# Residual sums that stay on the chip as the next layer's input, with their squares; normalisation moved into the next projection, chunk by chunk; the first token mixture in two VectorE passes

## The chip, the cores and the metric

The kernel runs on one core of one Trainium2 chip. The metric is the time of one execution on the device in microseconds (us); of three runs of the kernel before, the median is 6700.87 us.

## What is computed

Four layers work on 256 context tokens and 1024 latent tokens of 1024 channels in float32. The layers' mixers are RWKV-7 (layer 0), neighbourhood attention (layer 1), S5 (layer 2) and RWKV-7 again (layer 3). Around each mixer:

```python
for i in range(DEPTH):
    hx = _rms_norm(x, norm_g[i]) * (1.0 + scale_x) + shift_x
    hc = _rms_norm(ctx, norm_g[i]) * (1.0 + scale_c) + shift_c
    ...                                    # oc, ox = mixer(hc, hx)
    x = x + gate_x * ox
    if need_ctx:
        ctx = ctx + gate_c * oc
```

`_rms_norm` divides by the root of the mean square over the channels. Scale, shift and gate come from a modulation matrix and differ between context and latents. The RWKV mixer starts with six mixtures of each token with its neighbours: `xx = _centred_shift(h) - h` (the centred shift is half the sum of the left and the right neighbour), then `xs = h + xx * mu[n]` for n = 0 to 5, each followed by a projection.

## The kernel before

Channels lie on the 128 partitions in eight tiles (KT = 8), the 1280 tokens (T) along the free axis, the context first (SEGS). Matmuls work on three chunks of tokens, (0,512), (512,1024), (1024,1280) (CHUNKS), one PSUM bank each. In the last layer the first and the fourth projection need latents alone and use two chunks from token 256. The program is a row of phases. Each phase (class Phase, L57) opens a block in which every engine has its own instruction list, ordered by semaphores, and ends with a barrier of all engines (L83) and the clearing of its semaphores by GpSimd (L89). Nothing of the next phase starts before that barrier.

One layer runs through these phases. In RWKV layers `load_constants` (L112) loads eight small tensors. `norm` (L298) loads the residual stream from DRAM into h (SP, L312), squares each tile on ScalarE (L320), adds the squares over channels on TensorE with a matrix of ones (L337), forms the reciprocal root by Ln and Exp on ScalarE (L322, L324), multiplies h by it on VectorE (L348) and applies scale and shift on ScalarE (L328, once for the context and once for the latents). In layers 0 and 3 TensorE's list also has 147 and 17 instructions at its end that do nothing but count a semaphore (NORM_FILL). Then a projection phase multiplies h with strips of weights of 128 output channels: `rwkv_project` (L1580), `na_project` (L534) or `s5_prepare` (L950). Then the mixer (`rwkv_recur`, `na_attention`, or S5's scan and outputs), and at last `dense_residual` (L459), which multiplies the output with eight strips (L356), adds the gated product to the residual on VectorE (L507), and stores the sum to DRAM (L515). Its loop is a hardware loop of four turns with two strips each on every engine.

In `rwkv_project` VectorE prepares the first mixture group by group: neighbour sums (L1638), edge columns (L1642), `dd = 0.5*sum - h` (L1645) and `xs[0] = h + dd*mu` (L1631); after each group TensorE may use that chunk (xs_part, L1679). The five other mixtures are whole passes over 1280 columns. GpSimd in the meantime weighs the next layer's modulation strips (class HiddenModulation, L132; L153, L156), also in the projections of layers 1 and 2. In layer 3 there is no next layer and GpSimd is idle.

In `s5_prepare` VectorE and ScalarE work out the discretised states (L1176 to L1223 and on) while TensorE multiplies the first eight strips. In `na_project` SP loads eight pieces of value weights (L557) before the first two strips (L561). In `rwkv_recur` TensorE runs a loop over eight channel tiles, with an inner loop of five windows, both in hardware loops.

## Time and profile before

| | |
|---|---|
| runs | 6700.87 us median, 6697.97 to 6701.71 |
| span of the profiled execution | 6691.4 us |
| TensorE matmuls busy | 5726.3 us, 86% |
| VectorE busy | 2945.0 us, 44% |
| ScalarE busy | 2000.7 us, 30% |
| GpSimd busy | 1877.3 us, 28% |
| mean granted TensorE clock | 0.932 |
| HBM read and written | 329.14 MB, 105.87 MB |

The span is cut into phases by the barriers. Within it, a layer's norm phase is recognised by SP's eight loads of L312, and the following phase by its first instruction. The engines are named PE (TensorE), DVE (VectorE), ACT (ScalarE), POOL (GpSimd) and SP; a name with a q is the engine's sequencer or queue. A float32 matmul appears as two records.

### The profile page before, as it was taken

The page shows a single profiled execution, that of the slowest core. Times are in us where ns is not written, and L with a number is a line of the kernel's source. Part 1 is how long each engine was busy: PE and PEld are TensorE (multiplying, and loading weights), DVE is VectorE, ACT ScalarE, POOL GpSimd, SP SyncE. Part 2 cuts the span into 40 slices and gives each one's busy share as a digit, 9 for nine tenths or more (in the row PEclk, how much of TensorE's full clock was granted, in tenths as well). Part 3 has the DMA queues.
Part 4 walks back from the last instruction along what each step waited for, and adds up shares of the span by engine and source line. Part 5 has one row for each costly group of instructions (what it writes and reads, how often), then busy time and mean ns, then how long its engine had stood idle before and what let it go on. Part 6 is the DMA issues. An engine that isn't in the chain of part 4 may idle for free. (4 is left out here: it accounts for less than half of the span.)

```text
span 6691.4 us, 214952 instructions
## 1 busy us (share of the span) xinstructions
PE 5726.3 (86%) x92840; PEld 3836.5 (57%) x92840; DVE 2945.0 (44%) x6319; ACT 2000.7 (30%) x3323; POOL 1877.3 (28%) x2006
## 2 busy tenths in 40 slices
PE   5999888888887799977887885689799888888887
PEld 4555577777774355445554453544354477777773
DVE  6200266666662233135533377520310366666661
ACT  1000255555440222133422132310100254555440
POOL 4452144444441335100001641000000244444440
PEclk8999999999998899988898997899899899999998
DMA  3222100001102322122212236523112100011002
GB/s 125 89 96 82 50 31 31 31 33 43 37 31 85 121 76 97 46 85 64 62 48 103 97 104 92 122 73 115 52 68 75 47 31 31 31 44 39 31 31 91
DMA packets 196092, 441.22 MB, mean 66 GB/s; under 512 B 24769, under 2 KB 108609, under 8 KB 195649
## 3 DMA queue, kind: packets, MB, share of 16 engines
q1 hardware_dynamic: 160896, 338.58, 17.0%
q10 hardware_dynamic: 34752, 96.51, 3.6%
q8 instruction: 304, 4.98, 0.3%
q14 instruction: 140, 1.14, 0.1%
HBM read 329.14 MB, written 105.87 MB: 65 GB/s over the span
## 5 line engine op out<-in xcount | busy, mean ns | idle before, releaser
L356 PE MATMUL ps<-arena 128*128 128x512 f32 x4544 | 1683.6, 532 | 73.1 <-DMA arena<-s_w_in 27.4
L356 PEld LDWEIGHTS ps<-arena 128*128 128x128 f32 x4544 | 862.3, 190 | 889.7 <-issue 853.9
L1875 PE MATMUL ps<-arena 64*64 64x64 f32 x35840 | 741.3, 225 | 164.2 <-DVE arena L2542 66.1
L153 POOL TENSOR_TENSOR arena<-arena 128x512 f32<-128x512 f32 (+1 forms) x360 | 330.6, 935 | 1782.7 <-DMA arena<-w_mod 1772.5
L1875 PEld LDWEIGHTS ps<-arena 64*64 64x64 f32 x35840 | 646.8, 138 | 237.9 <-issue 223.9
L2280 ACT COPY arena<-ps 128x512 f32<-128x512 f32 (+1 forms) x880 | 536.0, 627 | 426.6 <-PE ps L1875 418.3
L2425 POOL TENSOR_TENSOR arena<-arena 128x256 f32<-128x256 f32 (+1 forms) x320 | 318.5, 1002 | 807.7 <-DVE arena L2666 528.9
L570 PE MATMUL ps<-arena 128*128 128x512 f32 (+1 forms) x1152 | 424.2, 528 | 33.5 <-DMA arena<-na_w_in 33.5
L2350 POOL MEMSET arena<- 128x1280 f32 (+4 forms) x22 | 15.1, 739 | 1370.6 <-POOLq L83 1370.6
L1631 DVE SCALAR_TENSOR_TENSOR arena<-arena 128x1280 f32<-128x1280 f32 (+3 forms) x120 | 147.2, 1299 | 567.2 <-PE ps L356 477.1
L156 POOL TENSOR_TENSOR arena<-arena 128x256 f32<-128x256 f32 (+2 forms) x504 | 381.8, 769 | 52.0 <-issue 2.1
L1696 ACT COPY arena<-ps 128x1280 f32<-128x1280 f32 (+1 forms) x64 | 75.0, 1172 | 1054.3 <-PE ps L356 749.0
L2542 DVE TENSOR_TENSOR arena<-ps,arena 128x512 f32<-128x512 f32 x486 | 319.5, 686 | 91.0 <-PE ps L1862 42.3
L570 PEld LDWEIGHTS ps<-arena 128*128 128x128 f32 x1152 | 219.9, 191 | 227.1 <-issue 215.9
L1679 PE MATMUL ps<-arena 128*128 128x512 f32 (+1 forms) x640 | 260.0, 568 | 96.2 <-DVE arena L1631 96.2
L507 DVE SCALAR_TENSOR_TENSOR arena<-ps,arena 128x1024 f32<-128x1024 f32 (+1 forms) x56 | 50.5, 937 | 507.4 <-PE ps L356 507.4
L1843 PE MATMUL ps<-arena 128*128 128x512 f32 (+1 forms) x432 | 225.9, 629 | 37.5 <-DMA arena<-rw_par 36.4
L653 DVE RECIPROCAL arena<-arena 128x1280 f32<-128x1280 f32 x16 | 130.5, 8154 | 288.2 <-ACT arena L615 288.2
L1679 PEld LDWEIGHTS ps<-arena 128*128 128x128 f32 x640 | 124.3, 195 | 230.3 <-issue 206.0
L2613 DVE TENSOR_TENSOR arena<-ps,arena 128x512 f32<-128x512 f32 x240 | 165.4, 689 | 166.7 <-ACT arena L2280 100.1
L2703 DVE SCALAR_TENSOR_TENSOR arena<-ps,arena 128x64 f32<-128x64 f32 x576 | 136.2, 278 | 227.6 <-PE ps L2089 218.1
L320 ACT ACTIVATE arena<-arena 128x1280 f32<-128x1280 f32 x32 | 40.6, 1270 | 593.3 <-DMA arena<-xres 489.7
(258 smaller groups left out, 9853.6 us busy)
## 6 DMA issues: line engine op xcount, KB each, us to landing
arena<-proj SPq DMA_DIRECT2D x158, 640.0 KB, 5.1
proj<-arena ACTq DMA_DIRECT2D x80, 640.0 KB, 4.0
arena<-w_mod SPq DMA_DIRECT2D x96, 512.0 KB, 7.6
arena<-rw_w SPq DMA_DIRECT2D x68, 512.0 KB, 3.7
arena<-xres SPq DMA_DIRECT2D x40, 640.0 KB, 6.7
xres<-arena ACTq DMA_DIRECT2D x24, 640.0 KB, 6.0
arena<-na_w_in SPq DMA_DIRECT2D x24, 512.0 KB, 3.5
arena<-x SPq DMA_DIRECT2D x16, 640.0 KB, 6.6
```

The source lines that it names most:

```text
L153: self.nc.gpsimd.tensor_tensor(out, strip[:, c:c + n, :], self.k.cond[:, c:c + n, s:s + 1].to_broadcast([P, n, P]), ALU.mult)
L156: self.nc.gpsimd.tensor_tensor(out, a, b, ALU.add)
L356: last = nc.tensor.matmul(k.ps[:, 3 * u + n, 0:b - a], w[:, c * P:(c + 1) * P], src[:, c, a:b], start=(c == 0), stop=(c == KT - 1))
L570: last = PE.matmul(k.ps[:, 3 * (s % 2) + n, 0:b - a], strips_[:, s % 2, c * P:(c + 1) * P], h[:, c, a:b], start=(c == 0), stop=(c == KT - 1))
L1631: return V.scalar_tensor_tensor(xs[n % 2][:, c, a:b], dd[:, c, a:b], k.mu[:, (j * 6 + n) * KT + c:(j * 6 + n) * KT + c + 1], h[:, c, a:b], ...
L1679: last = nc.tensor.matmul(k.ps[:, 3 * u + m, 0:b - a], strips_[:, u, c * P:(c + 1) * P], xs[0][:, c, a:b], start=(c == 0), stop=(c == KT - 1))
L1843: PE.matmul(lora_bank(banks, i), w2t[:, 2 * which + s, :], hid[:, which, a:b], start=True, stop=True).then_inc(lora_mm, 1)
L1875: last = PE.matmul(part_of(out, dst, hh, g, d), part(l, src, hh, g, d), rhs, start=True, stop=True)
L2280: SC.copy(out, in_).then_inc(ev, 1)
L2425: return GP_.tensor_tensor(eighths(out), eighths(in_), k.eye2.unsqueeze(1).to_broadcast([P, out.shape[1] // C, C]), ALU.add)
L2542: return V.tensor_tensor(out.rearrange("p (h g q) -> p h g q", h=2, g=2), in_.rearrange("p h (g q) -> p h g q", g=2), flat(mask).unsqueeze ...
L2613: return V.tensor_tensor(out.rearrange("p (h q c) -> p h q c", h=2, c=C), in_.rearrange("p h (q c) -> p h q c", c=C), k.eye2.unsqueeze(1). ...
```

## The change

Four things change together.

1. `dense_residual` writes the residual sum into k.h, a fixed place at the top of SBUF that is kept until the next projection; it still stores it to DRAM, since the next residual addition reads it there. In the first three layers ScalarE squares each finished tile and VectorE adds it into k.acc (T columns). The hardware loop is written out as eight strips.
2. The norm phases and their loads are gone, and NORM_FILL with them. Ahead of layer 0 a new phase `first_squares` loads x into k.h and sums its squares in the same way, before the constants of the layer are loaded.
3. The class Normalised runs at the head of each projection phase: three matmuls with ones over k.acc, then Ln and Exp for each of three pieces of tokens, the multiplications on VectorE and scale and shift on ScalarE piece by piece. TensorE waits for a piece before the first strip's chunk of it (attention and S5); in RWKV VectorE waits before its neighbour sums. A piece in RWKV is one token longer where a neighbour is needed.
4. In RWKV the first mixture is `xs[0] = (1-mu)*h` on ScalarE, then `xs[0] += (mu/2)*sum` on VectorE. `dd = 0.5*sum - h` is made after all groups, in one pass over 1280 columns. The tile block hid now shares one tile with dd, so ScalarE waits for the sixth mixture before it writes hid.

```diff
-NORM_FILL = {0: 147, 3: 17}
...
+class Normalised:
+    def __init__(self, nc, k, es, layer, pieces):
+        self.nc, self.k, self.layer, self.pieces = nc, k, layer, pieces
+        self.sums, self.root, self.scaled, self.ready = (es.semaphore("nm_" + n) for n in ("sums", "root", "scaled", "ready"))
+    def tensor_part(self, pe):
+        for a, b in CHUNKS:
+            self.nc.tensor.matmul(self.k.psf[:, 3 * BANK + a:3 * BANK + b], self.k.ones, self.k.acc[:, a:b], start=True, stop=True).then_inc(self.sums, 1)
+    def scalar_roots(self, act):
+        for a, b in self.pieces:
+            act.wait_ge(self.sums, len(CHUNKS))
+            rstd = self.k.acc[:, a:b]
+            self.nc.scalar.activation(rstd, self.k.psf[:, 3 * BANK + a:3 * BANK + b], ACT.Ln, bias=self.k.eps, scale=1.0 / D)
+            act.drain()
+            self.nc.scalar.activation(rstd, rstd, ACT.Exp, scale=-0.5).then_inc(self.root, 1)
+    def vector_part(self, dve, m):
+        a, b = self.pieces[m]
+        dve.wait_ge(self.root, m + 1)
+        for c in range(KT):
+            h = self.k.h[:, c, a:b]
+            self.nc.vector.tensor_tensor(h, h, self.k.acc[:, a:b], ALU.mult).then_inc(self.scaled, 1)
+    def scalar_part(self, act, m, c):
+        a, b = self.pieces[m]
+        act.wait_ge(self.scaled, m * KT + c + 1)
+        for s, (lo, hi) in enumerate(SEGS):
+            lo, hi = max(lo, a), min(hi, b)
+            if lo < hi:
+                h = self.k.h[:, c, lo:hi]
+                last = self.nc.scalar.activation(h, h, ACT.Identity, bias=self.k.mod[:, self.layer * MODS + c, s:s + 1],
+                                                 scale=self.k.mod[:, self.layer * MODS + 8 + c, s:s + 1])
+        return last.then_inc(self.ready, 1)
+    def wait_ready(self, eng, m, c=KT - 1):
+        eng.wait_ge(self.ready, m * KT + c + 1)
+def first_squares(nc, k, src):
...
-        @block.tensor
-        def _(pe):
-            for c in range(KT):
-                pe.wait_ge(sq_done, c + 1)
-                for n, (a, b) in enumerate(CHUNKS):
-                    last = nc.tensor.matmul(k.ps[:, n, 0:b - a], k.ones, sq[:, c % 2, a:b],
-                                            start=(c == 0), stop=(c == KT - 1))
-                last.then_inc(mm_done, 1)
-            for _ in range(NORM_FILL.get(layer, 0)):
-                hold(k, pe)
+                    act.wait_ge(added, c - 1)
+                nc.scalar.activation(sq[:, c % 2, :], k.h[:, c, :], ACT.Square).then_inc(sq_done, 1)
         @block.vector
         def _(dve):
-            dve.wait_ge(root_done, 1)
             for c in range(KT):
-                dve.wait_ge(x_in[c], 16)
-                nc.vector.tensor_tensor(h[:, c, :], h[:, c, :], rstd, ALU.mult).then_inc(scaled, 1)
-def strip_matmuls(nc, k, u, w, src, chunks=CHUNKS):
+                dve.wait_ge(sq_done, c + 1)
+                if c == 0:
+                    nc.vector.tensor_copy(k.acc, sq[:, 0, :]).then_inc(added, 1)
+                else:
+                    dve.wait_ge(added, c)
+                    nc.vector.tensor_tensor(k.acc, k.acc, sq[:, c % 2, :], ALU.add).then_inc(added, 1)
+def strip_matmuls(nc, k, u, w, src, chunks=CHUNKS, before=None):
 
     for n, (a, b) in enumerate(chunks):
+        if before:
+            before(n)
         for c in range(KT):
...
+            for c in range(KT):
+                u = c % 2
+                if c >= 2:
+                    sp.wait_ge(mm_done, c - 1)
+                sp.dma_start(strips[:, u, :], weights[c]).then_inc(w_in[u], 16)
+                if c >= 2:
+                    sp.wait_ge(ev_done, c - 1)
+                sp.dma_start(xin[:, u, first:T], src[c][:, first:T]).then_inc(x_in[u], 16)
 
...
+            def add_squares(c):
+                dve.wait_ge(sq_done, c + 1)
+                if c == 0:
+                    nc.vector.tensor_copy(k.acc, sq[:, 0, :]).then_inc(added, 1)
+                else:
+                    dve.wait_ge(added, c)
+                    nc.vector.tensor_tensor(k.acc, k.acc, sq[:, c % 2, :], ALU.add).then_inc(added, 1)
+
+            for c in range(KT):
+                u = c % 2
+                dve.wait_ge(mm_done, c + 1)
+                dve.wait_ge(x_in[u], c // 2 * 16 + 16)
+                for s, (a, b) in list(enumerate(SEGS))[int(latents):]:
+                    gate = k.mod[:, layer * MODS + 16 + c, s:s + 1]
+                    out, prod, x = k.h[:, c, a:b], acc(k, u)[:, a - first:b - first], xin[:, u, a:b]
+                    if chunked:
+                        out, x = (v.rearrange("p (j s) -> p j s", s=S) for v in (out, x))
+                        prod = acc(k, u).rearrange("p (s j) -> p j s", s=S)[:, a // S:b // S, :]
+                    last = nc.vector.scalar_tensor_tensor(out, prod, gate, x, ALU.mult, ALU.add)
+                last.then_inc(ev_done, 1)
+                if c and not latents:
+                    add_squares(c - 1)
+            if not latents:
+                add_squares(KT - 1)
 
...
+            for c in range(KT):
+                act.wait_ge(ev_done, c + 1)
+                act.dma_start(dst[c], k.h[:, c, first:T]).then_inc(stored, 16)
+                if not latents:
+                    if c >= 2:
+                        act.wait_ge(added, c - 1)
+                    nc.scalar.activation(sq[:, c % 2, :], k.h[:, c, :], ACT.Square).then_inc(sq_done, 1)
+            act.wait_ge(stored, 16 * KT)
...
+            normal.tensor_part(pe)
+
             def chunk(s, n):
                 a, b = CHUNKS[n]
+                if s == 0:
+                    normal.wait_ready(pe, n)
...
+            normal.scalar_roots(act)
+            for m in range(len(CHUNKS)):
+                for c in range(KT):
+                    normal.scalar_part(act, m, c)
...
+            for m in range(len(CHUNKS)):
+                normal.vector_part(dve, m)
...
+            normal.scalar_roots(act)
             act.wait_ge(par_in, 128)
             SC.activation(step, step, ACT.Exp).then_inc(stepped, 1)
+            for m in range(len(CHUNKS)):
+                for c in range(KT):
+                    normal.scalar_part(act, m, c)
...
+            for m in range(len(CHUNKS)):
+                normal.vector_part(dve, m)
...
+    groups = chunks_of(0) + [(0, tokens_of(0))][:tokens_of(0)]
+    kept_mixed = len(chunks_of(0))
+    pieces = [(a + (a > 0 and a != tokens_of(0)), b + (b < T and b != NCTX)) for a, b in groups]
...
+            mu = k.mu[:, j * 6 * KT:(j * 6 + 1) * KT]
+            V.tensor_scalar(half_mu, mu, 0.5, None, ALU.mult)
+            V.tensor_scalar(less_mu, mu, -1.0, 1.0, ALU.mult, ALU.add)
+            dve.drain().then_inc(mu_split, 1)
             edges = [t for a, b in SEGS for t in ((a, a + 1), (b - 1, b - 2))]
-            for a, b in chunks_of(0) + [(0, tokens_of(0))][:tokens_of(0)]:
+            normal.vector_part(dve, 0)
+            for m, (a, b) in enumerate(groups):
                 lo, hi = max(a, 1), min(b, T - 1)
                 for c in range(KT):
+                    normal.wait_ready(dve, m, c)
                     V.tensor_tensor(dd[:, c, lo:hi], h[:, c, lo - 1:hi - 1], h[:, c, lo + 1:hi + 1], ALU.add)
                 dve.drain()
                 for t, beside in edges:
                     if a <= t < b:
                         V.tensor_copy(dd[:, :, t:t + 1], h[:, :, beside:beside + 1])
                 dve.drain()
-                for c in range(KT):
-                    V.scalar_tensor_tensor(dd[:, c, a:b], dd[:, c, a:b], 0.5, h[:, c, a:b], ALU.mult, ALU.subtract)
-                dve.drain()
-                if a >= tokens_of(0):
+                if m < kept_mixed:
                     for c in range(KT):
-                        last = mix(0, c, a, b)
+                        dve.wait_ge(kept_part, m * KT + c + 1)
+                        last = V.scalar_tensor_tensor(xs[0][:, c, a:b], dd[:, c, a:b], half_mu[:, c:c + 1], xs[0][:, c, a:b], ALU.mult, ALU.add)
                     last.then_inc(xs_part, 1)
+                if m + 1 < len(groups):
+                    normal.vector_part(dve, m + 1)
+            dve.drain()
+            for c in range(KT):
+                V.scalar_tensor_tensor(dd[:, c, :], dd[:, c, :], 0.5, h[:, c, :], ALU.mult, ALU.subtract)
+            dve.drain()
...
+            normal.scalar_roots(act)
+            act.wait_ge(mu_split, 1)
+            for m, (a, b) in enumerate(groups):
+                for c in range(KT):
+                    normal.scalar_part(act, m, c)
+                if m < kept_mixed:
+                    act.wait_ge(normal.ready, (m + 1) * KT)
+                    for c in range(KT):
+                        nc.scalar.activation(xs[0][:, c, a:b], h[:, c, a:b], ACT.Copy, scale=less_mu[:, c:c + 1]).then_inc(kept_part, 1)
...
+            act.wait_ge(xs_ready, 5)
...
+        first_squares(nc, k, src)
...
```

The rest of the diff moves addresses in SBUF, takes the removed arguments out of calls and deletes `dense_to_dram`, which nothing calls.

## Rows read from the trace of the kernel before

**Rows 1.** Waits of TensorE, whole span: total us, times, longest us

```profile
PE ps L337 <- ACT arena L320: 49.8, 4, 16.1
```

**Rows 2.** Timeline, layer 0 to 1: start us, us, engine, line, operation, out<-in, [idle <-releaser]

```profile
2212.01 1.68 DVE L507 SCALAR_TENSOR_TENSOR arena<-ps,arena 128x256 f32<-128x256 f32 x2 [15.35 <-PE ps L356]
...
2217.30 4.62 SPq L312 DMA_DIRECT2D arena<-xres  x8
...
2247.24 13.10 ACT L328 ACTIVATE arena<-arena 128x256 f32<-128x256 f32 x16 [1.56 <-DVE arena L348]
2260.59 4.79 SPq L557 DMA_DIRECT2D arena<-na_w_v  x8
...
2275.15 5.47 PE L570 MATMUL ps<-arena 128*128 128x512 f32 x6 [33.45 <-DMA arena<-na_w_in]
```

**Rows 3.** Timeline of ACT, squares of the norm phase of layer 1

```profile
2226.72 1.27 ACT L320 ACTIVATE arena<-arena 128x1280 f32<-128x1280 f32 x1 [2.26 <-PE ps L337]
2228.87 1.27 ACT L320 ACTIVATE arena<-arena 128x1280 f32<-128x1280 f32 x1 [0.89 <-PE ps L337]
```

**Rows 4.** Timeline of ACT, roots of the same norm phase

```profile
2241.73 1.33 ACT L322 ACTIVATE arena<-ps,arena 128x1280 f32<-128x1280 f32 x1 [1.68 <-PE ps L337]
2243.11 1.28 ACT L324 ACT_TABLE_LOAD   x1
2244.41 1.27 ACT L324 ACTIVATE arena<-arena 128x1280 f32<-128x1280 f32 x1
```

**Rows 5.** Groups by form, 4650 to 4762 us: busy us, mean ns of one, idle

```profile
L348 DVE TENSOR_TENSOR arena<-arena 128x1280 f32<-128x1280 f32 x8 | 11.3, 1488 | 38.2 <-ACT arena L324 38.2
L1631 DVE SCALAR_TENSOR_TENSOR arena<-arena 128x512 f32<-128x512 f32 x16 | 10.8, 746 | 0.2
...
L328 ACT ACTIVATE arena<-arena 128x1024 f32<-128x1024 f32 x8 | 9.8, 1226 | 0.0
...
L328 ACT ACTIVATE arena<-arena 128x256 f32<-128x256 f32 x8 | 4.7, 586 | 1.6 <-DVE arena L348 1.6
```

**Rows 6.** Timeline, layer 1 to 2: norm loads and first projection matmuls

```profile
3589.20 0.83 SPq L312 DMA_DIRECT2D arena<-xres  x2
...
3641.14 36.97 PE L356 MATMUL ps<-arena 128*128 128x512 f32 x96 [27.42 <-DMA arena<-s_w_in]
```

**Rows 7.** Timeline, layer 2 to 3: norm loads and TensorE's second chunk

```profile
4666.55 4.15 SPq L312 DMA_DIRECT2D arena<-xres  x8
...
4742.20 28.20 PE L1679 MATMUL ps<-arena 128*128 128x512 f32 x58 [6.10 <-DVE arena L1631]
```

**Rows 8.** Timeline around layer 0: SP, DVE, GpSimd and TensorE

```profile
72.84 0.34 SPq L120 DMA_DIRECT2D arena<-m_x  x1
...
78.55 4.20 SPq L312 DMA_DIRECT2D arena<-x  x8
...
124.04 4.89 DVE L1638 TENSOR_TENSOR arena<-arena 128x511 f32<-128x511 f32 x8 [4.76 <-PEq L83]
...
155.68 5.52 POOL L156 TENSOR_TENSOR arena<-arena 128x256 f32<-128x256 f32 x5
...
168.48 30.75 PE L1679 MATMUL ps<-arena 128*128 128x512 f32 x80 [13.32 <-DVE arena L1631]
```

**Rows 9.** Stretch of layer 0's norm: us, engines busy, PEclk, DMA share, GB/s

```profile
92.00:94.00 2.00, 2.00 (x7) 1.08 (x6) 0.00 (x0) 1.11 (x2) 0.00 (x0) 1.00 0.44 182
```

**Rows 10.** Groups by form, 78 to 200 us: neighbour sums beside GpSimd

```profile
L1638 DVE TENSOR_TENSOR arena<-arena 128x512 f32<-128x512 f32 x8 | 9.3, 1226 | 0.0
```

**Rows 11.** Timeline of DVE, evictions of layer 0's residual (third in rows 2)

```profile
2177.60 1.68 DVE L507 SCALAR_TENSOR_TENSOR arena<-ps,arena 128x256 f32<-128x256 f32 x2 [15.35 <-PE ps L356]
2194.98 1.68 DVE L507 SCALAR_TENSOR_TENSOR arena<-ps,arena 128x256 f32<-128x256 f32 x2 [15.71 <-PE ps L356]
```

**Rows 12.** DMA queues, one tile of the recurrence, 1047 to 1201 us: packets, MB

```profile
q8 instruction: 14, 0.23, 0.7%
```

**Rows 13.** Waits of TensorE in the same tile

```profile
PE ps L1875 <- issue: 5.1, 8, 2.3
```

More of the change, by code:

```diff
@@ L40, in __init__, with hold_h @@
     def __init__(self, tensor, cols):
-        self.tensor, self.cols, self.at = tensor, cols, 0
+        self.tensor, self.all, self.cols, self.at = tensor, cols, cols, 0
+    def hold_h(self, held):
+        self.cols = self.all - KT * T * held
     def take(self, *shape):
@@ L300, in norm @@
+def first_squares(nc, k, src):
     sq = k.arena.take(2, T)
-    rstd = k.arena.take(T)
     with Phase(nc) as es:
-        sem = lambda n: es.semaphore(n)
-        x_in = [sem(f"x_in{c}") for c in range(KT)]
-        sq_done, mm_done, root_done = sem("sq_done"), sem("ss_mm"), sem("root_done")
-        scaled, final = sem("scaled"), sem("final")
+        x_in = [es.semaphore(f"x_in{c}") for c in range(KT)]
+        sq_done, added = es.semaphore("sq_done"), es.semaphore("sq_added")
         block = es.block()
@@ L478, in _ @@
         def _(sp):
-            with sp.Fori(0, n) as i:
-                for u in range(2):
-                    sp.wait_ge(mm_done[u], i + 1)
-                    sp.dma_start(strips[:, u, :], dram_tile(weights, i * 2 + u)).then_inc(w_in[u], 16)
-                    sp.wait_ge(ev_done[u], i + 1)
-                    sp.dma_start(xin[:, u, first:T], dram_tile(src, i * 2 + u)[:, first:T]).then_inc(x_in[u], 16)
+            for c in range(KT):
[6 more added lines that the diff above has]
+                sp.dma_start(xin[:, u, first:T], src[c][:, first:T]).then_inc(x_in[u], 16)
@@ L486, in _ @@
         @block.tensor
         def _(pe):
-            with pe.Fori(0, n) as i:
-                for u in range(2):
-                    pe.wait_ge(w_in[u], i * 16 + 16)
-                    pe.wait_ge(ev_done[u], i + 1)
-                    strip_matmuls(nc, k, u, strips[:, u, :], o, chunks).then_inc(mm_done[u], 1)
+            for c in range(KT):
+                u = c % 2
+                pe.wait_ge(w_in[u], c // 2 * 16 + 16)
+                if c >= 2:
+                    pe.wait_ge(ev_done, c - 1)
+                strip_matmuls(nc, k, u, strips[:, u, :], o, chunks).then_inc(mm_done, 1)
@@ L947, with s5_prepare @@
 LAGS = 2 * S - 1
-def s5_prepare(nc, k, s5, h, weights, z_d, mod_layer):
-    take = k.arena.take
+def s5_prepare(nc, k, s5, weights, z_d, mod_layer):
+    take, h = k.arena.take, k.h
     strips, stage = take(2, KT * P), take(2, S * NG)
@@ L1665, in _ @@
         def _(pe):
+            normal.tensor_part(pe)
             for n in range(4):
```

174 lines of the change are left out of this document (46 added, 128 removed).

## The prediction

> **What bounds the kernel now.** I read the waits by engine first, then the order of time around each norm phase, then the instruction groups by form inside it. TensorE is busy 86% of the span, so the change can gain only where TensorE stands still or works for the norm. The waits name one such place directly: the norm phases' first squares hold it for 49.8 us in four waits [rows 1]. The timeline shows how long the whole hole is. After the first layer the last residual product is evicted at 2212.0 (two DVE instructions, 1.7 us), the norm phase starts to load the residual at 2217.3, the modulation of h (ACT) ends at 2260.3, and the next projection's first matmul starts at 2275.15 [rows 2]. Most of those 63 us are one serial chain, and the same chain stands before every layer. So the sum is made at four places, and each time from the first instruction of a phase, which I call T0, to the matmul from which TensorE runs on. The profiled execution spans 6691.4 us; its time outside the span is taken as 9.5 us, which puts it on the median of 6700.87.
>
> **What a projection costs at its head now.** The new class runs at the head of a projection: three matmuls with ones, then three pairs of Ln and Exp, then the multiplications on DVE and the modulation on ACT, chunk by chunk. All of it is priced from before.
> Matmuls: TensorE comes from standing idle, as it did for the first squares of the norm phase. There one tile's three matmuls held ACT until 2226.7, 4.1 us from their start, against a pitch of 2.15 us from then on [rows 3]. I take 4.1 (range 2.1 to 4.1) and end at T0+4.4.
> Roots: Ln at 2241.73, a table load of 1.28, Exp at 2244.41 lasting 1.27 [rows 4]. For 512 columns each activation shrinks to about 0.6, for 256 to 0.35. The first load is hidden behind the matmuls. First pair 2.6, second 3.85 with its own loads, third 3.35: T0+7.0, T0+10.8, T0+14.2. ACT does all three before its first modulation, so splitting costs about 4.7 us here, and DVE's multiplications of the first chunk (8 x 0.61, as the sums of 511 columns in [rows 8]) are finished before ACT is free.
> The trace shows the next activation 0.02 us after the load [rows 4]. The Trainium skill, ScalarE: Activation LUTs, section What ACT_TABLE_LOAD costs, states a drain of 1.38 us beside each load; by that the five exposed loads would cost 6.9 us more at each of four places and the time would be near 6605. The trace does not agree, and I go by the trace.
> Modulation: 0.587 us for 256 columns and 1.226 for 1024, overlapping 0.09 [rows 5], so pitches of 0.50, 0.71 (512, interpolated) and 1.14. A first chunk that straddles context and latents needs 16 pieces of 256: 8.1 us, T0+22.3. The later chunks take 5.7 and 4.0, less than the 6.8 to 10 us that TensorE needs per chunk, so they stay hidden.
>
> **The four places.**
> Before layer 1 (attention): T0 becomes the old start of the norm phase, 2217.3, plus 0.2. Square and the last addition follow the last eviction (DMA issue 0.35, Square 1.27, addition 1.49 as a DVE pass over 1280 columns [rows 5], so 2217.1), while the last store lands at about the same time; 0.2 is the difference, between 0 and 3. TensorE starts at 2217.5+22.3 = 2239.8 instead of 2275.15: **35.3**. The weights (4 MB of value weights queued ahead on SP) needed 14.5 us, so they no longer end the wait.
> Before layer 2 (S5): T0 = 3589.4, one small Exp before the modulation adds 0.3, start 3612.1 instead of 3641.14 [rows 6]: **29.0**. DVE's discretisation now starts about 25 us into the phase. Its result is needed only after eight strips (8 x 17 us), so I cost the delay at nothing; if that cover were gone it would cost the 20 us or so by which DVE starts later.
> Before layer 3 (RWKV): constants load as now, T0 = 4666.55+0.2 [rows 7]. The pieces lie in one segment, so modulation is 5.7: T0+19.9. The neighbour sums trail (T0+20.5), edges 0.4, ACT makes (1-mu)h at 0.6 to 0.7 a tile beside DVE's second pass of 0.67: first chunk at T0+26.3. Second chunk: multiplications 4.9, sums 4.9, edges and drains 0.4, mixture 5.4, serial on DVE: T0+41.9. What counts is when TensorE may run on with its second chunk: now 4742.20 [rows 7], then 4708.65: **33.6**. One full pass (0.5(sum)-h) is gone here and comes back later over 1280 columns (11.8 us), beside eight strips of matmuls, of which none waits for it.
> Before layer 0 (RWKV): the new phase with squares starts where constants load now, at 72.84. Its loads ended by 93, that is 14.4 after the first was issued [rows 8, 9], so here at 87.3; Square, addition and the way out give 90.5. Constants add 5.7: T0 = 96.2 against 124.04. GpSimd works until 161.2, 37 us into the phase, and beside it a DVE pass over 512 columns takes 1.22 us instead of 0.61 [rows 8, 10]. Chunk one: modulation T0+22.3, sums until 24.6, mixture at 1.22: T0+35.0. Chunk two: mostly free of GpSimd, 5.5+5+5.5: T0+51.0 = 147.2, against 168.48 now [rows 8]: **21.3** (8 to 25 by how much of DVE's work GpSimd slows).
> Residual products: the loop is written out. Evictions are 17.38 us apart over a jump and 17.03 within a turn [rows 11]; three jumps in each of four layers give **4.2** (0 to 4.4). Squares and additions, 1.27 and 1.49 us per 17 us strip, hide behind the matmuls. If they were exposed they would cost 2.8 per strip.
> Sum 35.3+29.0+33.6+21.3+4.2 = 123.4, and 6700.9-123.4 = **6577.5 us**.
>
> **The rivals.**
> The head costs more than I add up: matmuls, roots, drains, modulation and DVE queue one behind another with a few semaphore hops each. For it: four engines alternate over three chunks. Against: every duration is measured. 5 to 12 us at each place: 6598 to 6625, middle 6610.
> One load serves both functions: the Trainium skill, ScalarE: Activation LUTs, section Table sets: the hidden batching unit, names a set that holds exp and ln. As a mechanism of this kernel it drops the five exposed loads of 1.28 us, 6.4 us at each of four places, which gives 6552. The trace shows a load ahead of both, so it speaks against it.
> The recurrences shift: TensorE's stream loses 147 and 17 fillers and gains unrolled matmuls, so the tile loop starts elsewhere in the instruction memory. In one tile 14 instruction packets arrive and TensorE stands 5.1 us for "issue" [rows 12, 13]. Doubled over 16 tiles: +82, 6660. Halved: 6537. The two layers sit at different offsets now and look alike, which speaks for little effect.
> Slower than before: the inner window loop, 1684 instructions as counted in the program (seven or eight packets of 256), is no longer kept and is fetched again in four more turns. 28 packets at 5.1/14 = 0.36 us are 10 us a tile, 164 us in all, more than the gain: 6741. It decides from 7.7 us a tile. Against: seven or eight packets hold it wherever it starts. The Trainium skill, Runtime: NRT & Kernel Launch, section Instruction fetch mechanics, puts TensorE's memory at 128 KiB, which is eight such packets, and says that a taken branch out of the window stalls; no row here gives the size.
> It does nothing: TensorE's start is set by weights. Attention's 14.5 us after T0 stay below 22.3, so this would need the loads to slow down by half.
>
> **How the numbers follow.** Forecast (6560 to 6597) 0.70; costlier head 0.13; shift by up to +82 or -40 0.08; one table set 0.05; slower 0.02; nothing 0.02. The range 6548 to 6622 reaches over the first two cases, one table set and the unknown bounds (matmuls at the pitch of 2.15 us -8, store and additions +8, GpSimd +13, jumps +4). A measurement can tell about 0.2%, 13 us, from no change. Faster 0.95, same 0.02, slower 0.03.
>
> **What would show it.** No matmuls or loads of a norm phase; six table loads in a row at each head; TensorE's first projection matmul 22 us after the phase starts in attention and S5, second chunk at 42 and 51 us in RWKV; evictions 17.0 apart everywhere; tiles of the recurrence within 1 us of now. Wrong if modulation starts later than 15 us into a phase, or if a tile changes by over 2 us.

## The result: 5.6% slower, and where the time went

| | before | after |
|---|---|---|
| median of the runs | 6699.42 us (6696.94 to 6701.71, 4 runs) | 7075.81 us (7072.59 to 7083.38, 4 runs) |
| ratio, 95% interval | | 1.0564, 1.0551 to 1.0577 |
| span of the profiled execution | 6691.4 us | 7081.5 us |

The forecast was 6577.5 with a range of 6548 to 6622. These lines are from the page of the changed kernel: the span, the busy sums, the rows of slices for TensorE and its granted clock, and the queue of instruction packets (packets, MB, share).

```profile
span 7081.5 us, 214110 instructions
...
PE 5788.8 (82%) x92672; PEld 3901.0 (55%) x92672; DVE 2986.5 (42%) x6387; ACT 2066.1 (29%) x3451; POOL 1883.9 (27%) x2006
...
PE   5999788888878999788988759899966776767667
...
PEclk8999899999989999888989879999988888898888
...
q8 instruction: 606, 9.93, 0.6%
```

The last quarter of the span is thin: TensorE's tenths are mostly 6 and 7 there. That is layer 3's recurrence. The instruction queue brought 606 packets; before it was 304.

**The heads.** Timeline of the changed kernel at the head of attention (columns as in rows 2). T0 is 2197.97.

```profile
2192.81 1.68 DVE L466 SCALAR_TENSOR_TENSOR arena<-ps,arena 128x256 f32<-128x256 f32 x2 [14.13 <-PE ps L382]
2194.40 1.48 DVE L454 TENSOR_TENSOR arena<-arena 128x1280 f32<-128x1280 f32 x1
...
2196.20 1.49 DVE L454 TENSOR_TENSOR arena<-arena 128x1280 f32<-128x1280 f32 x1 [0.32 <-ACT arena L481]
2197.97 3.81 SPq L523 DMA_DIRECT2D arena<-na_w_v  x8
...
2198.01 4.60 PE L312 MATMUL ps<-arena 128*128 128x512 f32 x6 [5.24 <-PEq L88]
...
2202.66 0.69 ACT L318 ACTIVATE arena<-ps,arena 128x512 f32<-128x512 f32 x1 [3.40 <-PE ps L312]
...
2203.40 1.28 ACT L320 ACT_TABLE_LOAD   x1
2204.70 0.63 ACT L320 ACTIVATE arena<-arena 128x512 f32<-128x512 f32 x1
...
2212.76 12.90 ACT L336 ACTIVATE arena<-arena 128x256 f32<-128x256 f32 x23
...
2220.87 4.69 PE L540 MATMUL ps<-arena 128*128 128x512 f32 x6 [18.25 <-ACT arena L336]
```

From the last eviction to the projection's first matmul it is 28.06 us; before it was 63.14 [rows 2]. The same reading at the other places (the earlier one in each pair is the eviction, or in layer 0 the span's own clock):

```profile
3533.85 1.68 DVE L466 SCALAR_TENSOR_TENSOR arena<-ps,arena 128x256 f32<-128x256 f32 x2 [14.13 <-PE ps L382]
...
3561.40 4.60 PE L382 MATMUL ps<-arena 128*128 128x512 f32 x5 [18.40 <-ACT arena L336]
```

```profile
4575.61 1.68 DVE L466 SCALAR_TENSOR_TENSOR arena<-ps,arena 128x256 f32<-128x256 f32 x2 [14.13 <-PE ps L382]
...
4586.39 4.22 PE L312 MATMUL ps<-arena 128*128 128x512 f32 x6 [10.81 <-PEq L88]
...
4628.33 2.08 PE L1681 MATMUL ps<-arena 128*128 128x512 f32 x2 [6.00 <-DVE arena L1644]
```

```profile
123.07 9.86 DVE L1644 SCALAR_TENSOR_TENSOR arena<-arena 128x512 f32<-128x512 f32 x8
...
133.08 10.10 PE L1681 MATMUL ps<-arena 128*128 128x512 f32 x16 [31.27 <-DVE arena L1644]
148.94 2.07 PE L1681 MATMUL ps<-arena 128*128 128x512 f32 x2 [5.76 <-DVE arena L1644]
```

The four heads gain 35.1 + 29.7 + 33.7 + 19.5 = 118.0 us, where 119.2 were forecast. At layer 3's second chunk the changed kernel is 4742.20 - 4628.33 = 113.9 us ahead [rows 7]; the other 4.1 went between the heads. So up to there the change does what it says.

**The loss.** From that matmul to the recurrence's first tile both kernels need 538 us. Then they part. SP loads the parameters of the next channel tile once per turn of the recurrence. Its issues in layer 3, first in the kernel before, then in the changed one:

```profile
5280.26 0.47 SPq L1811 DMA_DIRECT2D arena<-rw_par  x1
5402.08 0.44 SPq L1811 DMA_DIRECT2D arena<-rw_par  x1
5553.69 0.39 SPq L1811 DMA_DIRECT2D arena<-rw_par  x1
...
6469.36 0.55 SPq L1811 DMA_DIRECT2D arena<-rw_par  x1
```

```profile
5166.60 0.44 SPq L1823 DMA_DIRECT2D arena<-rw_par  x1
5337.00 0.45 SPq L1823 DMA_DIRECT2D arena<-rw_par  x1
5553.76 0.37 SPq L1823 DMA_DIRECT2D arena<-rw_par  x1
...
6843.70 0.44 SPq L1823 DMA_DIRECT2D arena<-rw_par  x1
```

That is (6469.36 - 5402.08) / 7 = 152.5 us a tile before and (6843.70 - 5337.00) / 7 = 215.2 after. In layer 0 it is 153.2 before and 153.5 after. The eight intervals cost 1677.1 against 1189.1 us, 488.0 more, and what follows the last issue 15.8 more; less the 113.9 gained that is the 390 us between the spans.

One tile of layer 3 in both, as a stretch (us, busy time of PE, PEld, DVE, ACT and POOL with counts, granted clock, DMA share, GB/s), before and after:

```profile
5402.10:5553.70 151.60, 131.72 (x4825) 113.15 (x4819) 99.34 (x193) 76.17 (x133) 66.66 (x68) 0.98 0.10 35
```

```profile
5553.80:5771.50 217.70, 152.02 (x4782) 127.90 (x4782) 98.53 (x192) 76.22 (x132) 67.80 (x67) 0.84 0.08 26
```

The work is the same, and no other engine does noticeably more. TensorE stands for 65.7 us in place of 19.9, and its matmuls take 20.3 us longer at a mean granted clock of 0.84 in place of 0.98. These two tiles are the extremes in granted clock. Over all seven tiles TensorE's busy time rises from 133.4 to 148.5 us a tile, 15.1 of the 62.8, at granted clocks of 0.84 to 0.91 in place of 0.94 to 0.98; the other 47.7 are time in which it stands. In the changed kernel's tile 50 instruction packets arrive (13 in the same tile before), and TensorE's waits begin with "issue", where [rows 13], a tile of layer 0, had 5.1 us:

```profile
q8 instruction: 50, 0.82, 1.7%
```

```profile
PE ps L1887 <- issue: 35.2, 17, 5.1
PE ps L1874 <- issue: 8.4, 5, 2.8
PE ps L1928 <- issue: 6.5, 5, 2.0
```

It is TensorE's own code, fetched again and again: the rival that the prediction gave 0.02.

### The profile page after: what moved, and what is told of

It reads as the page before. It is cut to its first block and busy times, and to the rows that moved or that the text cites. A ratio compares the mean times of both kernels' runs of the same rounds, so it can differ in the third digit from the quotient of the medians.

```text
span 7081.5 us, 214110 instructions
## 1 busy us (share of the span) xinstructions
PE 5788.8 (82%) x92672; PEld 3901.0 (55%) x92672; DVE 2986.5 (42%) x6387; ACT 2066.1 (29%) x3451; POOL 1883.9 (27%) x2006
## 3 DMA queue, kind: packets, MB, share of 16 engines
q8 instruction: 606, 9.93, 0.6%
## 5 line engine op out<-in xcount | busy, mean ns | idle before, releaser
L1887 PE MATMUL ps<-arena 64*64 64x64 f32 x35840 | 792.7, 233 | 428.1 <-issue 330.0
L1887 PEld LDWEIGHTS ps<-arena 64*64 64x64 f32 x35840 | 684.7, 145 | 474.5 <-issue 462.0
L2362 POOL MEMSET arena<- 128x1280 f32 (+4 forms) x22 | 15.1, 739 | 1331.5 <-POOLq L88 1331.5
L1622 DVE SCALAR_TENSOR_TENSOR arena<-arena 128x1280 f32<-128x1280 f32 (+1 forms) x80 | 118.1, 1550 | 555.6 <-PE ps L382 477.1
L1874 PE MATMUL ps<-arena 64*64 64x64 f32 x8832 | 208.0, 227 | 117.4 <-issue 73.9
L1874 PEld LDWEIGHTS ps<-arena 64*64 64x64 f32 x8832 | 176.1, 140 | 173.5 <-issue 173.4
```

The lines of the kernel that those rows point to most:

```text
L1874: last = PE.matmul(part_of(out, c ^ (hh & cross), hh, g, d), ops[HP[hh], l, d, at:at + C], ops[HP[hh], r, d, at:at + C], start=True, stop= ...
L1887: last = PE.matmul(part_of(out, dst, hh, g, d), part(l, src, hh, g, d), rhs, start=True, stop=True)
```

## The experiments

**Where the window loop lies.** The inner loop of five windows has 1685 instructions (the prediction had counted 1684). Its place can be counted in the compiled program, in packets of 256 instructions (a packet is 9.93 MB / 606 = 16.4 KB, and an instruction has 64 bytes in that program). In that count a float32 matmul is four instructions and a transpose two, and jumps that only lead on to the next block are left out. I write the offset of its first instruction in its packet. Before: 19 in layer 0, 233 in layer 3. After: 44 and 177. The change took 147 and 17 fillers out and wrote out a loop, which moved everything behind. 6.6 packets of code can touch seven packets or eight. The theory takes the program in the chip's memory to sit further on by an unknown constant K: the loop is kept if it touches seven packets as loaded, and fetched again at each of the four jumps back if it touches eight. The rivals: something in the new code of layer 3 (its addresses, the new sharing of tiles) slows the recurrence, or the fetches come from another loop.

**Fillers back in the changed kernel.** 56 fillers (semaphore counts, nothing computed) behind the last strip of the RWKV projection in layer 3 bring the loop back to 233. Nothing else changes.

```diff
                 strip_matmuls(nc, k, u, strips_[:, u, :], xs[u]).then_inc(mm_done[u], 1)
+            for _ in range({0: 0, 1: 56}[j]):
+                hold(k, pe)
```

> The changed kernel with 56 empty semaphore counts more in TensorE's list at the end of layer 3's projection, so that the five-turn window loop of layer 3's recurrence starts 233 instructions into a block of 256 as in the kernel before, instead of 177. Theory (place of the loop in TensorE's instruction memory): a tile of layer 3 takes 152.5 us again instead of 215, instruction packets fall from 606 to about 300, and the time to 7076 - 8 x 62.8 = 6574 us. Rival (the recurrence is slower through the new addresses of its data): nothing of that moves, 7076 us.

Measured: 6579.96 us (6573.86 to 6589.03, 4 runs), ratio to before 0.9822 (0.9806 to 0.9839). Layer 3's tiles take 153.3 us with 13 packets each. The page's queue row:

```profile
q8 instruction: 311, 5.10, 0.3%
```

56 instructions that compute nothing make the kernel 496 us faster. The rest of the change is worth 117.2 us, 1.8%. The time lands 2.5 us from the forecast; that is closer than the gain, which is 6 us short, because the kernel before ran at 6697.18 in this batch and not at the 6700.9 of the forecast.

**Only the displacement, in the kernel before.** 200 more fillers ahead of layer 3 put its loop at 177, with none of the change.

```diff
-NORM_FILL = {0: 147, 3: 17}
+NORM_FILL = {0: 147, 3: 217}
```

> The kernel before with 217 instead of 17 fillers in layer 3's norm phase: its window loop then starts 177 into a block, as in the changed kernel; nothing else is different. Theory (place of the loop): a tile of layer 3 takes about 215 us, about 600 instruction packets, 6701 + 502 = 7203 us. Rival (addresses of the data): 200 fillers cost some 3 us at most beside other engines, 6701 us.

Measured: 7215.16 us (one run), 216.2 us a tile in layer 3, 152.7 in layer 0. Waits of TensorE in a tile of layer 3 and its packets:

```profile
PE ps L1875 <- issue: 37.4, 18, 5.2
PE ps L1862 <- issue: 8.7, 5, 2.3
```

```profile
q8 instruction: 50, 0.82, 1.7%
```

With the run above this settles the cause from both sides: undoing the displacement removes the loss, and the displacement alone brings it. The new code in layer 3 has no measurable part in it.

**No fillers at all in the kernel before.** Loops at 128 and 69.

```diff
-NORM_FILL = {0: 147, 3: 17}
+NORM_FILL = {}
```

> The kernel before with its fillers on TensorE at the head of the RWKV projections left out (0 instead of 147 and 17). Nothing that is computed changes. Counted in the compiled program, the inner window loop of layer 0 then starts at offset 128 of its packet of 256 instructions, that of layer 3 at 69. Theory (TensorE keeps the loop only where it touches seven packets, and the program as loaded sits a constant K of instructions further on, K between 23 and 63 by the runs so far): layer 0 is no longer kept, its tiles go from 153 to about 216 us, 50 packets each instead of 14, and the time is near 7205. Layer 3 at 69 tells the constant: kept if K is at most 38 (7205 in all), not kept otherwise (near 7700). Rival (the penalty belongs to layer 3, because of where it lies in the program or what it works on, not to the offset): layer 0 stays at 153 a tile; near 6700.

Measured: 7508.21 us (one run). Layer 0 takes 225.0 us a tile with 50 packets, as expected: the penalty isn't bound to layer 3. But layer 3 at 69 came out at a level that the theory did not have, 183.5 us and 32 packets, so that the total lies between the two that were expected:

```profile
q8 instruction: 32, 0.52, 1.3%
```

```profile
PE ps L1875 <- issue: 17.6, 14, 3.7
```

**Nearer to the edge.** The changed kernel with fillers for both layers, loops at 60 and 215.

```diff
+            for _ in range({0: 16, 1: 22}[j]):
+                hold(k, pe)
```

> The kernel after with 16 fillers on TensorE ahead of layer 0's recurrence and 22 ahead of layer 3's: window loops start at offsets 60 and 215. Theory with K between 23 and 63: layer 0 is kept if K is at most 47, layer 3 if K is at least 41. So either both are kept (K 41 to 47; near 6580), or exactly one is not (near 7080), never both. Rival (no sharp edge, the cost grows with how many instructions stick out of seven packets): tiles at some value between 153 and 216 us, with packets between 14 and 50.

Measured: 6816.02 us (one run). Layer 3 at 215 is kept (153.3 us, 13 packets), layer 0 at 60 isn't: 182.0 us, 32 packets. "Exactly one of the two" held, so K is at least 48; that the one lost lies between the levels speaks for the rival in part. It is not a slope, though. All seven full tiles have 32 packets, as at 69. In 50 - 14 = 36 extra packets each of the four jumps brings nine, in 32 - 14 = 18 two of the four do. The trace shows which two. A turn of the window loop ends with the products of L2058. These are the ends of turns one to four in one tile of layer 0:

```profile
1175.77 1.61 PE L2058 MATMUL ps<-arena 64*64 64x128 f32 x25 [0.32 <-ACT arena L2294]
...
1195.69 1.98 PE L2058 MATMUL ps<-arena 64*64 64x128 f32 x32 [0.32 <-ACT arena L2294]
...
1225.96 1.61 PE L2058 MATMUL ps<-arena 64*64 64x128 f32 x25 [0.32 <-ACT arena L2294]
...
1246.17 1.98 PE L2058 MATMUL ps<-arena 64*64 64x128 f32 x32 [0.32 <-ACT arena L2294]
```

So turns two, three and four take 19.9, 30.3 and 20.2 us, and no, nine and no instruction packets arrive in them; turn five, which ends at 1278.43, takes 32.3 us and brings nine. After every second jump back the loop is fetched again, and the turns between run at nearly the 19.3 us of a kept turn. In the changed kernel's layer 3 turns two to five bring nine packets each and take 32 to 35 us. So the fetches belong to the window loop and to no other. Why every second turn is spared at this level, no row shows.

**A longer loop at good offsets.** The kernel with 56 fillers, with 109 more inside the loop (1794 instructions, two more than seven packets) and both offsets kept at 44 and 233; for that the 56 ahead of layer 3's recurrence become 203, since layer 0's loop is longer too.

```diff
-            for _ in range({0: 0, 1: 56}[j]):
+            for _ in range({0: 0, 1: 203}[j]):
                 hold(k, pe)
...
                 pe.wait_ge(xt_ev, it + 1)
-                hold(k, pe)
+                for _ in range(110):
+                    hold(k, pe)
```

> The kernel with 56 fillers, with 109 more fillers inside the window loop, which then has 1794 instructions, two more than seven packets, and starts at the same offsets as in the kernel with 56 fillers (44 and 233), where it was kept in both layers. Theory (seven packets are kept, eight are not): now neither layer is kept: about 50 packets and 215 us or more a tile in both, 14 packets before; near 7580, plus what 109 fillers in each of 80 turns cost by themselves (up to some 2 us a turn, 160 us). Rival (only the start offset decides, or eight packets can be kept): both layers stay at 14 to 16 packets a tile, and the time is 6580 plus only what the fillers cost, at most 6740.

Measured: 8475.14 us (one run). Layer 0 has 50 packets and 280.8 us a tile, layer 3 32 packets and 260.8 us. So length counts, not the start alone, and eight packets are not kept. Layer 3 came out at the 32-packet level and not at the 50 expected, with an eighth packet touched by few instructions. The price of the fillers was missed by far: beside 225.0 us (50 packets) and 183.5 (32) in the kernel without fillers they cost 56 and 77 us a tile, 0.10 and 0.14 us for each of 545, against the 0.02 that I had allowed. In the tile of layer 0 below TensorE's longest wait for issue is 21.0 us; 109 fillers in a row feed it nothing.

```profile
PE ps L1889 <- issue: 113.6, 15, 21.0
```

**The two edges against each other.** All of this fits one constant K between 48 and 63: seven packets touched, kept; an eighth touched by up to about 40 instructions, 32 packets; by 69 or more, 50. Then the upper edge of the good offsets lies at 107 - K and the lower one at 256 - K, and a kernel at 52 and 201 has one loop on either side.

```diff
+            for _ in range({0: 8, 1: 16}[j]):
+                hold(k, pe)
```

> The kernel after with 8 fillers on TensorE ahead of layer 0's recurrence and 16 ahead of layer 3's: window loops start at offsets 52 and 201 (counted in the compiled program). Theory in the form that all runs so far allow (the loop is kept where it touches seven packets; as loaded everything sits K instructions further, K between 48 and 63; where it touches an eighth by a few instructions, two of four jumps back fetch it again, 32 packets and 182 us a tile; where by 68 or more, all four, 50 packets and 215 to 225 us): one of the two edges lies on each side. K up to 54: layer 0 kept at 153, layer 3 at 215 with 50 packets, near 7080. K from 56: layer 0 at 182 with 32 packets, layer 3 kept at 153, near 6815. K of 55: both kept. Rival (the two edges are unrelated thresholds of the offset, not the two ends of one span of seven packets): both layers kept without K being 55, or both fetched again, is possible; near 6580 or near 7300.

Measured: 6805.82 us (one run). Layer 0 at 52 is lost with 32 packets and 179.8 us, layer 3 at 201 is kept with 13 and 153.9. That is the branch "K from 56", with its time of 6815. K is 56 to 63, and the changed kernel's layer 0 at 44 is kept by at most seven instructions. There is a single run for most offsets, but the packets leave no doubt of the level. K itself is a fit and nothing in the record shows it directly. The runs alone put the stretch of good offsets between 100 wide (201 to 44 are kept) and 130 (177 and 52 are lost); the 108 that seven packets leave to a loop of 1685 lie within.

| offset, length | us a tile | packets | touched as loaded (K = 56 to 63) |
|---|---|---|---|
| 201, 215, 233, 19, 44; 1685 | 152.5 to 154.2 | 13, 14 | seven |
| 52, 60, 69; 1685 | 180, 182, 183 | 32 | eight, by 1 to 25 |
| 233; 1794 | 261 with fillers | 32 | eight, by 35 to 42 |
| 128, 177; 1685 | 225, 215 to 216 | 50 | eight, by 77 or more |
| 44; 1794 | 281 with fillers | 50 | eight, by 102 or more |

**The mixture in three passes again.** The kernel with 56 fillers, with `dd = 0.5*sum - h` and then the mixture back in each group on VectorE, and without ScalarE's (1-mu)h.

```diff
+                for c in range(KT):
+                    V.scalar_tensor_tensor(dd[:, c, a:b], dd[:, c, a:b], 0.5, h[:, c, a:b], ALU.mult, ALU.subtract)
+                dve.drain()
                 if m < kept_mixed:
                     for c in range(KT):
-                        dve.wait_ge(kept_part, m * KT + c + 1)
-                        last = V.scalar_tensor_tensor(xs[0][:, c, a:b], dd[:, c, a:b], half_mu[:, c:c + 1], xs[0][:, c, a:b], ALU.mult, ALU.add)
+                        last = mix(0, c, a, b)
...
-            dve.drain()
-            for c in range(KT):
-                V.scalar_tensor_tensor(dd[:, c, :], dd[:, c, :], 0.5, h[:, c, :], ALU.mult, ALU.subtract)
...
-                if m < kept_mixed:
-                    act.wait_ge(normal.ready, (m + 1) * KT)
-                    for c in range(KT):
-                        nc.scalar.activation(xs[0][:, c, a:b], h[:, c, a:b], ACT.Copy, scale=less_mu[:, c:c + 1]).then_inc(kept_part, 1)
```

> As fill56, but with the first mixture of RWKV in three VectorE passes again (sum, half sum less h, mixture, chunk by chunk) and without ScalarE's part of it. If VectorE's serial passes set when TensorE may run on, two passes over 512 columns come back in layer 3 (2 x 4.9 us) and two in layer 0, the first beside GpSimd (9.8 + 4.9): 25 us more than fill56, about 6599 us. If ScalarE's passes set it, the time stays or falls by up to 5 us.

Measured: 6604.17 us (6599.34 to 6613.12, 4 runs), ratio to before 0.9864 (0.9848 to 0.9881), 24 us more than with two passes. Layer 3's head, where the extra pass stands in the chain:

```profile
4608.84 5.64 DVE L1635 TENSOR_TENSOR arena<-arena 128x512 f32<-128x512 f32 x8 [3.32 <-ACT arena L336]
...
4614.82 4.91 DVE L1642 SCALAR_TENSOR_TENSOR arena<-arena 128x512 f32<-128x512 f32 x8
4619.81 5.39 DVE L1622 SCALAR_TENSOR_TENSOR arena<-arena 128x512 f32<-128x512 f32 x8
```

The 4.91 us stand in the chain of each of two chunks, and layer 3's second chunk comes 10.0 us later in its phase. Layer 0's second chunk starts at 159.10 in place of 148.69, 10.4 us and not the 14.7 expected. The extra pass does take 9.87 us beside GpSimd, but it pushes the mixture behind it out of GpSimd's time, which then takes 5.89 us in place of 9.86. So VectorE's serial passes do set when TensorE runs on, and the fourth part of the change is worth some 24 of the 117 us, 20 of them seen at these two places.

**The order of the roots.** Four of the six table loads of 1.28 us a head are avoidable: all three Ln, then all three Exp, needs two. First everywhere, in the kernel with 56 fillers:

```diff
+        act.wait_ge(self.sums, len(CHUNKS))
         for a, b in self.pieces:
-            act.wait_ge(self.sums, len(CHUNKS))
+            self.nc.scalar.activation(self.k.acc[:, a:b], self.k.psf[:, 3 * BANK + a:3 * BANK + b], ACT.Ln, bias=self.k.eps, scale=1.0 / D)
+        act.drain()
+        for a, b in self.pieces:
             rstd = self.k.acc[:, a:b]
-            self.nc.scalar.activation(rstd, self.k.psf[:, 3 * BANK + a:3 * BANK + b], ACT.Ln, bias=self.k.eps, scale=1.0 / D)
-            act.drain()
             self.nc.scalar.activation(rstd, rstd, ACT.Exp, scale=-0.5).then_inc(self.root, 1)
```

> As fill56, but the three Ln stand together and then the three Exp, so two table loads a head instead of six, one of them hidden. If ScalarE's chain of roots sets the start of the modulation, each of the four heads is 5.1 us shorter (four exposed loads of 1.28): 20 us less than fill56, about 6554 us. If VectorE or the landing weights set TensorE's start, no difference.

Measured: 6571.56 us (6570.49 to 6578.53, 4 runs), ratio to before 0.9812 (0.9796 to 0.9829); 8 us less than with 56 fillers where 20 less was expected, and the intervals overlap. The heads say more. Attention and S5 start 5.7 and 5.0 us earlier in their phases. Layer 3's second chunk gains only 3.3 and layer 0's loses 0.6. The first root comes later, since it waits for all three Ln, and in layer 0 VectorE's first multiplications then take 8.51 us beside GpSimd in place of 7.66. So the next kernel orders by place: three and three in attention and S5, the first pair alone and then two and two in layer 3, layer 0 as it was.

```diff
+        for group in {0: ((0,), (1,), (2,)), 3: ((0,), (1, 2))}.get(self.layer, (tuple(range(len(self.pieces))),)):
+            ...                  # Ln of the group, drain, Exp of the group
```

> The kernel with 56 fillers, with ScalarE's order of the roots changed by place: all three Ln ahead of all three Exp in attention and S5 (two table loads a head), first pair alone and then Ln Ln Exp Exp in layer 3 (four loads), three pairs as they are in layer 0 (six). If the per-place readings of the grouped kernel hold (5.7 and 5.0 us in attention and S5, 3.3 in layer 3, nothing in layer 0): 14 us less than with 56 fillers, 6566 against 6580, ratio between the two 0.998. Rival (the gains at the heads are given back in what follows, so that only the scatter of the recurrences showed): no difference from 56 fillers.

> The kernel with 56 fillers once more, beside the one with the order of the roots changed, on the same chip: 6580, 0.982 of the time before.

Measured, on one chip: 6573.80 us (6569.23 to 6579.35, 5 runs), ratio 0.9814 (0.9800 to 0.9827), against 6588.12 (6576.92 to 6594.87, 5 runs), ratio 0.9833 (0.9819 to 0.9846). The intervals overlap from 0.9819 to 0.9827, so the totals alone only suggest a gain, though four of the five runs with 56 fillers lie above all five of the others. The difference of 14.3 us is close to the sum expected from the places, and so are the starts. These are attention's ScalarE and its first projection matmul, which starts 17.1 us after the phase in place of 22.9:

```profile
2196.18 1.28 ACT L318 ACT_TABLE_LOAD   x1 [1.81 <-PEq L88]
2200.86 1.63 ACT L318 ACTIVATE arena<-ps,arena 128x512 f32<-128x512 f32 x3 [3.40 <-PE ps L312]
2202.55 1.28 ACT L322 ACT_TABLE_LOAD   x1
2203.84 1.46 ACT L322 ACTIVATE arena<-arena 128x512 f32<-128x512 f32 x3
...
2213.35 2.90 PE L542 MATMUL ps<-arena 128*128 128x512 f32 x3 [12.53 <-ACT arena L338]
```

This version and the one with all roots grouped are the fastest measured, 1.9% faster than before.

## The prediction's steps against the measurement

The working of the heads held almost to the microsecond. "Measured" is the changed kernel's trace; each gain is from the last eviction (in layer 0 from the span's start) to the matmul that the prediction named.

| step | forecast | measured |
|---|---|---|
| attention, T0 to first matmul | 22.3 | 22.90 |
| gain before layer 1 | 35.3 | 63.14 - 28.06 = 35.1 |
| gain before layer 2 | 29.0 | 57.21 - 27.55 = 29.7 |
| layer 3, T0 to second chunk | 41.9 | 41.9 |
| gain before layer 3 | 33.6 | 86.45 - 52.72 = 33.7 |
| layer 0, second chunk at | 147.2 | 148.94 |
| gain before layer 0 | 21.3 | 19.5 |
| residual loops written out | 4.2 | about 0 |
| tiles of the recurrence, layer 0 and layer 3 | within 1 us | +0.4, +62.8 |

A tile that changes by over 2 us was one of the prediction's own signs of being wrong.

**Heads.** Matmuls with ones 4.6 (forecast 4.1), each Ln 0.69 (0.47 for 256 columns) and each load 1.28 with nothing behind it, six in a row, modulation of the first chunk in attention 8 us. The Trainium skill, ScalarE: Activation LUTs, section What ACT_TABLE_LOAD costs, adds a drain of 1.38 us to each load; the changed kernel's trace shows the Exp 0.02 us behind the end of its load, so going by the trace was right. The costlier head and the one table set both fall: no extra queueing of 5 to 12 us, and a load before every change of function. In layer 0 the first mixture pass took 9.86 us beside GpSimd, as priced (8 x 1.22), and the first chunk came at 133.1, 35.8 us after the phase began.

**Residual loops.** The mis-sized term. [rows 11] show 17.38 us, and the turn inside is 17.01 in the trace of before (2091.78 to 2108.79), but written out the strips do not come every 17.03. Two intervals of the changed kernel:

```profile
2072.38 1.68 DVE L466 SCALAR_TENSOR_TENSOR arena<-ps,arena 128x256 f32<-128x256 f32 x2 [23.77 <-PE ps L382]
2089.59 1.68 DVE L466 SCALAR_TENSOR_TENSOR arena<-ps,arena 128x256 f32<-128x256 f32 x2 [15.53 <-PE ps L382]
2106.79 1.68 DVE L466 SCALAR_TENSOR_TENSOR arena<-ps,arena 128x256 f32<-128x256 f32 x2 [14.79 <-PE ps L382]
```

17.21 and 17.20 are the mean of the old 17.01 and 17.38, and the seven intervals of a layer take 120.4 us in place of 120.2. So a jump costs TensorE nothing that shows here; a difference between two intervals on VectorE was read as a cost on TensorE's path. Squares and additions are hidden, as forecast.

**The failed step** is the sentence against the slower rival: "seven or eight packets hold it wherever it starts". The step was wrong: seven are kept and eight are not, so the offset decides. The rival of the shift (0.08) named the displacement too, with a cost of at most 82 us, and was set aside because the two layers "sit at different offsets now and look alike". That was weak support. Those are 19 and 233, both within the stretch of good offsets, which by the fit above is 108 of 256 wide. Had I counted the changed program's offset, 177, and set it beside 19 and 233, it would have been outside what the trace of before covers, with the kernel's own 17 and 147 fillers as a hint that position matters. By the same fit 148 of 256 offsets lose the loop. For one loop moved to an unknown place that is a chance of 0.58, and for two loops a chance of 0.82 that at least one is lost, not 0.02. That layer 0's loop stayed good at 44, seven instructions or fewer from the edge, was luck.

The Trainium skill, Runtime: NRT & Kernel Launch, section Instruction fetch mechanics, gives TensorE 128 KiB, refilled in blocks of 256 instructions (16 KiB), so eight blocks. By that, a loop of eight would fit if nothing else had to; here it is not kept, and seven are. The same section of the Trainium skill says that prefetch is sequential, and that a taken branch whose target lies outside the current window of two pages forces a fetch. By that window a loop over seven blocks would be fetched again at each jump as well. The trace does not agree: in tiles where the loop is kept only 13 or 14 packets arrive, and none in turns two to five. A sequential prefetch of one block past the loop would explain why the eighth place is not free. That is only argued; the nine packets per jump agree with it, and it does not explain why every second jump is spared at 32 packets.

**Its price** was too small as well: 28 packets at 0.36 us, 10 us a tile. Measured: 37 packets more in layer 3 and 62.8 us, 1.7 us a packet. [rows 12, 13] show packets that arrive in a stream of which most was hidden; a packet that the engine stands for costs more. And a quarter of the loss is no wait at all: over the seven tiles the matmuls themselves took 15.1 of the 62.8 us, at the lower granted clock. Where the rival had 164 us for both layers, it is 488.0 + 15.8 = 504 us for one.

**What remains.** Without the displacement the gain is 117 us in one batch of runs and 110 in another, against 123.4 forecast. Of the difference 4.2 us are the residual loops and 1.2 the heads. From its first projection matmul to its last eviction the attention layer took 1313.0 us in the changed kernel and 1308.8 before; its variants range from 1306.9 to 1322.9, so that is scatter as far as these runs tell. The recurrences of the changed kernels take 153.3 to 153.9 us a tile in layer 3 where it is kept, against 152.5 in the one profile of before: 6 to 10 us over seven tiles, with 0.95 to 0.96 granted clock in both. Whether that is scatter or belongs to the change stays open.

## What to carry to other kernels

Before an edit adds or removes instructions ahead of a large hardware loop, count where the loop lands in packets of 256 in the program of its engine, and compare that with the offsets at which it is known to run well. Instructions in a kernel that do nothing may be there for this. Only TensorE's loop was measured here. When one stage becomes slower with unchanged busy work, look at the packets of the instruction queue per turn and at waits for "issue" first. Test an edit's worth with the displacement undone: here 5.6% slower and 1.8% faster are the same edit, 56 instructions apart.

## What the runs showed of the hardware

- In all runs TensorE kept the window loop over its jumps back where, by the fit with K = 56 to 63, it touches seven packets of 256 instructions (five offsets of a loop of 1685), and did not where it touches eight (five offsets, and two of a loop of 1794). Extra packets per tile: 36 or 37 (nine at each of four jumps), or 18 or 19 (nine at every second jump) where the eighth is touched by 1 to 42 instructions. Cost of the loop of 1685: 27 to 31 us a tile at the lower level, 63 to 72 us at the upper.
- The runs fit a place in the chip's memory that lies 56 to 63 instructions (modulo 256) past the place counted in the compiled program, in this one program and its variants.
- Mean granted clock of a tile with the loop of 1685: 0.92 to 0.98 where it is kept, 0.89 to 0.93 at 32 packets, 0.80 to 0.91 at 50. TensorE stands 66 of 218 us in one tile with 50 packets and 20 of 152 in one that is kept.
- A filler (a semaphore count) in TensorE's loop cost 0.10 to 0.14 us where 109 stand in a row, in a loop that is fetched again. No run has them in a loop that is kept.
- VectorE's multiplications take 7.66 us for eight passes over 513 columns beside GpSimd in layer 0, and 4.92 in layer 3, where GpSimd is idle; the mixture takes 9.86 and 5.39 us for eight passes over 512.
